# Row scatters in two halves of 64 places, and another order of the ranks over the places

## The reference

```python
g_p, g_idx = lax.top_k(softmax(ht @ w_rg + b_rg), 1)        # one group of 8 experts for each token
e_logits = (ht @ w_re + b_re)[token, g_idx]
e_top, e_idx = lax.top_k(e_logits, 2)                        # two experts in the group
weights = g_p * softmax(e_top)
y = (silu(xb @ w_gate[e]) * (xb @ w_up[e])) @ w_down[e]      # for the rows xb of expert e; w_gate, w_up: 1024 x 256, w_down: 256 x 1024
out = zeros.at[token].add(weights * y)
result = rmsnorm(x + out)
```

## Time and profile before

| what | us |
|---|---|
| median of 3 runs | 1301.35 (1301.12 to 1304.85) |
| time of the profiled execution | 1302.32 |
| its span, first to last instruction | 1300.0 |
| PE busy | 1267.6 (98%) |
| DVE, ACT, POOL busy | 613.1, 460.4, 535.5 |
| moved by DMA | 211.38 MB |
| of it by POOL's queue | 8.29 MB in 5184 packets |

### The profile page before, as it was taken

One profiled execution on the slowest core, in us unless ns is written; L12 is line 12 of the kernel. 1 busy time (PEld: TensorE's weight loads), 2 busy tenths in 40 slices (PEclk: granted clock), 3 DMA queues, 4 the chain that ended last, 5 costly groups with the idle time before them and its releaser, 6 DMA issues.

```text
span 1300.0 us, 18634 instructions
## 1 busy us (share of the span) xinstructions
PE 1267.6 (98%) x6670; PEld 968.7 (75%) x6670; DVE 613.1 (47%) x1162; ACT 460.4 (35%) x770; POOL 535.5 (41%) x685
## 2 busy tenths in 40 slices
PE   8999999999999999999999999999999999999986
PEld 6767777787888888888888788777888875555552
DVE  4868768725542422222225765757243265222225
ACT  5657534435434324133144534145322210000102
POOL 4633323334555655555545664424644211121100
PEclk9999999999999999999999999999999999999999
DMA  7422222112334433434333333312426989999995
GB/s 221 107 65 56 66 58 66 50 49 81 98 96 113 131 97 97 130 98 129 97 98 114 97 93 85 83 49 67 128 81 268 362 323 394 424 421 424 424 423 240
DMA packets 212157, 211.38 MB, mean 163 GB/s; under 512 B 31903, under 2 KB 193425, under 8 KB 200817
## 3 DMA queue, kind: packets, MB, share of 16 engines
q1 hardware_dynamic: 203104, 200.25, 45.8%
q0 software_dynamic: 5184, 8.29, 1.7%
q10 hardware_dynamic: 3796, 1.86, 0.5%
HBM read 205.76 MB, written 16.78 MB: 171 GB/s over the span
## 4 chain that ended last, share of the span: by engine, by line
issue 39%; POOL 31%; PE 26%; DMA 1%; DVE 1%; POOLq 0%; ACT 0%; SPq 0%; DVEq 0%; ACTq 0%
POOL wlo L661 31%; PE bank L2287 8%; PE bank L2304 4%; PE bank L1915 3%; PE bank L1917 3%; PE bank L1916 3%; PE side L1945 2%; DMA y<-y_rows 1%; PE bank L1956 1%; DMA y_rows<-xe,tabi 1%; PE side L1917 1%; PE side L1915 1%; PE side L1916 1%; PE side L2203 1%; PE bank L2419 0%
## 5 line engine op out<-in xcount | busy, mean ns | idle before, releaser
L661 POOL TENSOR_TENSOR wlo<-raw,whi 128x256 fp32r<-128x256 f32 x644 | 498.2, 805 | 524.4 <-ACT whi L785 524.2
L1916 PE MATMUL bank<-actB_lo,whi 128*128 128x512 f32 x608 | 236.7, 389 | 0.0
L1915 PE MATMUL bank<-actB_hi,whi 128*128 128x512 f32 x576 | 227.7, 395 | 0.5 <-POOL wlo L661 0.5
L1917 PE MATMUL bank<-actB_hi,wlo 128*128 128x512 f32 x576 | 224.4, 390 | 0.0
L785 ACT ACTIVATE whi<-raw 128x1024 fp32r<-128x1024 f32 x161 | 169.0, 1051 | 151.8 <-PE bank L1917 124.9
L1915 PE MATMUL bank<-actA_hi,whi 128*128 128x512 f32 x400 | 157.3, 393 | 0.6 <-DVE actA_lo L1201 0.6
L1916 PE MATMUL bank<-actA_lo,whi 128*128 128x512 f32 x400 | 156.1, 390 | 0.0
L1917 PE MATMUL bank<-actA_hi,wlo 128*128 128x512 f32 x400 | 156.1, 390 | 0.0
L2287 PE MATMUL bank<-gu,xeT 128*64 128x256 f32 x1088 | 127.7, 384 | 4.7 <-issue 2.2
L1916 PEld LDWEIGHTS bank<-actB_lo,whi 128*128 128x128 f32 x608 | 114.2, 188 | 24.1 <-issue 1.0
L1915 PEld LDWEIGHTS bank<-actB_hi,whi 128*128 128x128 f32 x576 | 108.1, 188 | 25.9 <-issue 2.3
(11 more groups left out here) (433 smaller groups left out, 1653.0 us busy)
## 6 DMA issues: line engine op xcount, KB each, us to landing
dn<-in_w_exp_down SPq DMA_DIRECT2D x32, 1024.0 KB, 16.0
raw<-in_w_in SPq DMA_DIRECT2D x57, 512.0 KB, 3.8
gu<-in_w_exp_gate SPq DMA_DIRECT2D x28, 1024.0 KB
gu<-in_w_exp_up SPq DMA_DIRECT2D x28, 1024.0 KB
raw<-in_w_up SPq DMA_DIRECT2D x32, 512.0 KB, 3.9
raw<-in_w_down SPq DMA_DIRECT2D x32, 512.0 KB, 3.6
raw<-in_w_out SPq DMA_DIRECT2D x16, 512.0 KB, 3.7
raw<-in_w_in SPq DMA_DIRECT2D x16, 256.0 KB, 3.1
```

What stands on the lines that cost most here:

```text
L661: ins = nc.gpsimd.tensor_tensor(wlo[:, slot, at], raw[:, slot, at], whi[:, slot, at].bitcast(F32), ALU.subtract)
L1915: mm(b[:, :], w_hi, hi[:, k, :], start=first, stop=False)
L1916: mm(b[:, :], w_hi, lo[:, k, :], start=False, stop=False)
L1917: ins = mm(b[:, :], w_lo, hi[:, k, :], start=False, stop=last)
```

## The change

Only the scatters of rows are cut in two: one transfer for partitions 0 to 63 and one for partitions 64 to 127, each with 64 indices. The indices of the second are copied to a tile `tab_odd` in partitions 0 to 63, by two more DVE instructions (one in `list_values`, one in `list_overflow`). Each scatter now adds 32 to its semaphore instead of 16, and all waits on it are doubled. Gathers stay whole. The ranks are laid over the places in another order: place 4e + o takes rank 16o + e where o is even and 16o + 15 - e where it is odd (e = 0 to 15, o = 0 to 3), so that ranks 0 to 15 lie on 16 groups of four places, and so do the next 16. That takes 4 DVE instructions in place of 7.

```diff
+                                       ("tab_odd", [ROWS, EXTRA_AT + ODDS], I32))
...
+        def rows_landed(q):
+            return 16 * (q // X_BUFS + 1)
...
-                sp.wait_ge(S(f"scattered{j}"), 16 * LAST_E // 2)
+                sp.wait_ge(S(f"scattered{j}"), 32 * LAST_E // 2)
...
+            def whole(table, c):
+                return ((slice(0, P), tabi[:, table, c:c + 1]),)
+
+            def halves(c):
+                return (slice(0, ROWS), tabi[0:ROWS, 0, c:c + 1]), (slice(ROWS, P), tab_odd[:, c:c + 1])
+
+            def scatter(n, parts, done):
+                for at, slots in parts:
+                    pool.indirect_dma_start(y2_rows, bass.IndirectOffsetOnAxis(ap=slots, axis=0), xe[at, n, :], None,
+                                            bounds_check=slot_bound, oob_is_err=False).then_inc(done, 16)
...
-                scatter(q % X_BUFS, tabi[:, 0, q:q + 1], S(f"scattered{q % 2}"))
+                scatter(q % X_BUFS, halves(q), S(f"scattered{q % 2}"))
...
-                        pool.wait_ge(S(f"scattered{(q - 1) % 2}"), 16 * ((q - 1) // 2 + 1))
-                    gather(n % X_BUFS, tabi[:, 1, n:n + 1], S(f"gathered{n % X_BUFS}"))
+                        pool.wait_ge(S(f"scattered{(q - 1) % 2}"), 32 * ((q - 1) // 2 + 1))
+                    gather(n % X_BUFS, whole(1, n), S(f"gathered{n % X_BUFS}"))
...
-            ranks = const("iota")[:, 0:ROWS].rearrange("p (j b) -> p b j", b=8)
-            groups = rank_at.rearrange("p (b o) -> p b o", o=8)
-            for b in range(0, 8, 2):
-                chain(v.tensor_copy(groups[:, b:b + 2, b:8], ranks[:, b:b + 2, 0:8 - b]))
-                if b:
-                    chain(v.tensor_copy(groups[:, b:b + 2, 0:b], ranks[:, b:b + 2, 8 - b:8]))
+            ranks = const("iota")[:, 0:ROWS].rearrange("p (o e) -> p e o", e=16)
+            groups = rank_at.rearrange("p (e o) -> p e o", o=4)
+            for o in range(4):
+                if o % 2 == 0:
+                    chain(v.tensor_copy(groups[:, :, o:o + 1], ranks[:, :, o:o + 1]))
+                else:
+                    chain(v.tensor_scalar(groups[:, :, o:o + 1], ranks[:, :, o:o + 1], -1.0, float(32 * o + 15), ALU.mult, ALU.add))
...
-                chain(v.tensor_scalar(tabi[:, 0, FIRST], bank[2][:, 0:EXTRA_AT], float(SKIP), None, ALU.add), S("slots_ready"))
+                chain(v.tensor_scalar(tabi[:, 0, FIRST], bank[2][:, 0:EXTRA_AT], float(SKIP), None, ALU.add))
+                chain(v.tensor_copy(tab_odd[:, FIRST], tabi[ROWS:P, 0, FIRST]), S("slots_ready"))
...
+                units = slice(EXTRA_AT, EXTRA_AT + ODDS)
+                chain(v.tensor_copy(tab_odd[:, units], tabi[ROWS:P, 0, units]), S("over_listed"))
```

More of the change, by code:

```diff
@@ L364, in gated_blocks @@
         xeT, hidT, _ = lay(low_at, ("xeT", [P, 2, NK, P]), ("hidT", [P, 2, DE]))
-        tabi, over_n, steps64, over_at, spare_rows, tab_end = lay(low_at + words([P, 2, NK, P]) + words([P, 2, DE]),
+        tabi, over_n, steps64, over_at, spare_rows, tab_odd, tab_end = lay(low_at + words([P, 2, NK, P]) + words([P, 2, DE]),
                                        ("tabi", [P, 2, COLS], I32), ("over_n", [1, 2 * OVER + 1], I32), ("steps64", [P, 8]),
-                                       ("over_at", [P, 2], I32), ("spare_rows", [P, 1], I32))
+                                       ("over_at", [P, 2], I32), ("spare_rows", [P, 1], I32),
+                                       ("tab_odd", [ROWS, EXTRA_AT + ODDS], I32))
         below = place("below", [1, OVER, NE], b_at + words([P, X_BUFS, D]))
@@ L679, in _, with gather @@
             pool.wait_ge(S("rows_ready"), 1)
[L681 to L687, removed]
+            def whole(table, c):
+                return ((slice(0, P), tabi[:, table, c:c + 1]),)
+            def halves(c):
+                return (slice(0, ROWS), tabi[0:ROWS, 0, c:c + 1]), (slice(ROWS, P), tab_odd[:, c:c + 1])
+            def gather(n, parts, done):
+                for at, rows in parts:
+                    pool.indirect_dma_start(xe[at, n, :], None, x_rows, bass.IndirectOffsetOnAxis(ap=rows, axis=0),
+                                            bounds_check=row_bound, oob_is_err=False).then_inc(done, 16)
+            def scatter(n, parts, done):
+                for at, slots in parts:
+                    pool.indirect_dma_start(y2_rows, bass.IndirectOffsetOnAxis(ap=slots, axis=0), xe[at, n, :], None,
+                                            bounds_check=slot_bound, oob_is_err=False).then_inc(done, 16)
             def spare_expert():
@@ L701, in _ @@
             for q in range(X_BUFS - 1):
-                gather(q, tabi[:, 1, q:q + 1], S(f"gathered{q}"))
+                gather(q, whole(1, q), S(f"gathered{q}"))
             pool.wait_ge(S("slots_ready"), 1)
@@ L724, in overflow @@
                 pool.wait_ge(S("over_rows_set"), i)
-                gather((LAST_E - 1) % X_BUFS, over_at[:, 1:2], S("over_gathered"))
+                gather((LAST_E - 1) % X_BUFS, ((slice(0, P), over_at[:, 1:2]),), S("over_gathered"))
                 pool.wait_ge(S("over_y_made"), i)
@@ L729, in overflow @@
                 pool.wait_ge(S("over_slots_set"), i)
-                scatter((LAST_E - 1) % X_BUFS, over_at[:, 0:1], S("over_scattered"))
-            pool.wait_ge(S("scattered1"), 16 * LAST_E // 2)
+                scatter((LAST_E - 1) % X_BUFS, ((slice(0, P), over_at[:, 0:1]),), S("over_scattered"))
+            pool.wait_ge(S("scattered1"), 32 * LAST_E // 2)
             for_overflow(pool, over, overflow)
             for n in range(X_BUFS):
-                pool.wait_ge(S(f"gathered{n}"), 16 * ((LAST_E - n) // X_BUFS + 1))
+                pool.wait_ge(S(f"gathered{n}"), rows_landed(LAST_E - (LAST_E - n) % X_BUFS))
         def x_t_of(k):
@@ L1794, in list_overflow @@
                     chain(v.tensor_copy(tabi[rows, 0, to], slot))
-                    chain(v.tensor_copy(slotv[rows, :, to], table[:, 1:3, :]), S("over_listed") if rows == LOW_ROWS else None)
+                    chain(v.tensor_copy(slotv[rows, :, to], table[:, 1:3, :]))
+                units = slice(EXTRA_AT, EXTRA_AT + ODDS)
+                chain(v.tensor_copy(tab_odd[:, units], tabi[ROWS:P, 0, units]), S("over_listed"))
             rows_turned(0, 1)
@@ L2309, in turn_rows_of @@
             def turn_rows_of(q):
-                turn_rows(q % X_BUFS, S(f"gathered{q % X_BUFS}"), 16 * (q // X_BUFS + 1), 2 * q if q else None)
+                turn_rows(q % X_BUFS, S(f"gathered{q % X_BUFS}"), rows_landed(q), 2 * q if q else None)
             def down_landings(n):
```

## The result

The changed kernel takes 1307.18 us (median of 6 runs, 1304.94 to 1308.59) against 1301.6 us for the kernel before in the same measurement (1300.18 to 1304.85). The ratio is 1.004, 95% interval 1.0025 to 1.0054. It is slower by 0.4% (5.6 us, where 1.7 us less was forecast), outside the range. The profiled execution took 1304.94 us, its fastest; its span is 1303.0 us against 1300.0.

A forecast was written before the change was run, and what follows sets the result against it. DMA engines and PE are both full until 1266 us; the last scatter's landing sets the end. +0.7 - 0.78 = 0 before it, -2.2 + 0.5 = -1.7 after: 1301.35 - 1.7 = 1299.6 us, range 1296.8 to 1303.0.

The forecast's parts named there:

- Levelling: Half scatters spread rows over all 16 DMA engines; slowest engine ends 2.2 us earlier, bounds nothing to 3.3 us.
- rival B: Scatters: a 64-place transfer uses eight engines or the new order leaves the same skew; no levelling, 1302.7 us; chance 0.10.
- C: Queue q0 before the spare expert: a transfer costs as such, not by packet; slower, 1304.8 us; chance 0.09.
- its sign: What would show C: PE's stand at unit 9 grows by 2 us or more.
- The path to the end: After the last scatter lands, SP's loads come 1.7 us earlier and the rest follows, within PE's 1.99 us stand before block 2.
- the second half: Last scatter's second transfer, issued 1.31 us later on POOL; takes 0.5 us off the 2.2 us gain.
- Upper weights: PE's waits of 0.45 and 0.33 us for up weights near the end go: 0.78 us gained.
- Queue in the middle: Queue q0 before unit 9: 160 packets per scatter instead of 144 lengthen PE's stand by 0.5 us, bounds 0.3 and 2.8.
- The copy before `over_listed`: Gather of unit 4: one more DVE copy of 0.17 us, without cover, costs PE +0.2 us.
- gathered rows: Other gathers, issued 1.31 us later, stay hidden with 5.2 us in hand; uncovered, 1.3 us per unit.
- Ranks and tables: DVE instructions around 908 us and a copy after the values cost nothing; if uncovered, under 0.5 us.
- D's clock: Unit 15's down product: PE's clock stays up, so levelling counts whole, 1298.0 us, or 1296.4 without the other fall; chance 0.18.

The follow-up runs named there:

- second trace: A second profiled execution of the unaltered changed kernel, run again beside the kernel before: ratio 1.0038 (1.0023 to 1.0054).
- first trace: The first profiled execution of the changed kernel, against the kernel before: 1304.94 us, the fastest of its 6 runs.

## Why the prediction was wrong

**Levelling** is the step that failed. I took it that a transfer of 64 places gives each engine four neighbouring ones, counted 118 to 135 rows and got 1.4 us behind the mean. Nothing in the trace of before shows such a transfer, and I named no value for another deal. The packets of the last scatter show neighbours in pairs, on 16 engines, and the two parts run alone show that the order and the halves do harm only together: 76 to 177 rows by count, 8.1 us behind the mean, 7.9 us measured. In place of -2.2 us the slowest engine's end moved by +5.2 us (1274.7 to 1279.9).

**The bounds** failed with it. I bounded the levelling by nothing and 3.3 us, with no value below nothing; rival B had the right doubt, but took "no better than now" as its worst, 1302.7. C came nearest with its number, 1304.8, by another mechanism: its sign, a stand at unit 9 that grows by 2 us or more, did not show. The rule cited from the Trainium skill for B (DMA: Bandwidth & Descriptors, How many engines) says how many engines a transfer uses. The trace agrees: of each half the eight free engines take five packets each, 40 of 80, and the other eight the rest. It doesn't say which place goes to which engine, and I let it put B out. The formula cited from the Trainium skill (same page, The descriptor swizzle) is given for 128 partitions; I carried its groups of four over to 64.

**The path to the end.** I let everything hang on the last scatter, with 1.99 us of slack for the weights. In the profile after, the weights took 5.01 us and used it up; the second half (issue to issue 1.21 us, I had 1.31) was not what counted. In the second trace (weights +4.08, results loaded +3.87 us) the scatter's side sets the end, with a stand of 1.92 us. Both are late from the same eight engines.

**Upper weights.** I took 0.78 us off for PE's waits of 0.45 and 0.33 us. They became 1.36 and 1.23 us (1.36 and 0.79 in the second trace), and waits for gate weights came on top: the wrong sign. Such a wait costs nothing by itself, though: with the gather first on the kernel before, PE waits 1.33 us twice for up weights, at the time of before.

**Queue in the middle.** 160 packets per scatter came as counted (q0 has 5440 instead of 5184 in all, 16 scatters of 16 more). The stand at unit 9 went from 2.19 to 3.01 and 3.17 us in the two traces, 0.82 and 0.98 more, where I had 0.5 more and bounds of 0.3 to 2.8. But a stand there is worth nothing measurable at the end: 3.83 us and none at all both gave the time of before. That term should have been 0, and C, which rested on it, doesn't decide here.

**Small terms.** The copy before `over_listed` is there at 1083.89 (0.17 us); PE turned the rows at 1092.19 in the first trace and at 1091.44 in the second, against 1091.51, so +0.2 can't be told. After 1056 us PE never waited for gathered rows, as I had it. Ranks and tables cost nothing: the first gather is issued at 1049.38 and 1049.90, before at 1049.64. D's clock came true in one of the two traces (last down product but one in 3.65 us instead of 5.35), without any use, as the weights weren't there.

## What to carry to other kernels

A transfer's number of indices can decide which of its places share an engine, even where it uses the same 16 engines; when a transfer is cut, count the rows per engine anew under every deal that the trace leaves possible, and bound the gain by the worst of them. Where the engines are full for 100 us, unevenness adds up over all transfers and is paid at the end by whatever waits for all 16 parts of a load. A DMA share that stays at one half while work is left is the sign of it; a stand of PE in the middle of such a stretch may cost nothing. And a deal that predicts the right sign need not be the right one: p mod 16 did, and single packets of one transfer ruled it out.

## What the hardware showed unexpectedly

An indirect DMA of 64 places in partitions 0 to 63 or 64 to 127 uses 16 engines, 5 packets each (80 packets), and its rows fit engine = (place // 2) mod 16: two neighbours and, by the landings, the two that lie 32 further on. One of 128 places gave each half its own eight engines, and with the new order its free engines show three rows and an empty place, twice: four neighbours, and four more. POOL takes 0.90 us to issue a half scatter and 0.99 to 1.01 for a whole one, so a cut costs nearly a whole issue, 1.2 us with the gap. And one and the same kernel showed two courses, ACT starting 0.05 or 0.77 us behind the modelled end of PE's products in unit after unit, and the execution with the late start was the faster of the two (1304.94 against 1306.48 us).
